# Tokens of a dilated attention put in the order of their residue modulo 4, in a two-layer decoder kernel

## The chip, the cores and the metric

One core of one Trainium2 chip runs the whole kernel in one launch. The metric is the device time of one execution in microseconds (us); lower is better.

## The reference

Two decoder layers on 256 tokens of width 1024, in float32. Each layer adds a token mixer, then a mixture of 32 experts (top 2 of one group of 8), then a gated per-layer embedding. The mixer of layer 0 is the dilated attention (DSA) that the change is in; layer 1 has latent attention (MLA), which it doesn't touch.

The DSA has 8 heads of 128 columns, and each head three groups with their own q, k and v. A query at token t sees, in group g, the keys t, t-d, t-2d, ... down to t-window:

```
DSA_PATTERNS = ((128, 1), (512, 4), (2048, 16))      # (window, dilation) per group
s = where(valid, q.k * dh**-0.5 - slope * (t - key), -inf)
```

The three groups are joined by their softmax denominators, which is the same as one softmax over all keys of the three groups. Its result goes through w_out. With 256 tokens, groups 1 and 2 see only keys whose distance is a multiple of 4 and of 16; their windows reach past the first token.

## The kernel before

All five engines have their own written-out program, tied by semaphores. TensorE multiplies, ScalarE casts and takes exponentials, VectorE subtracts, scales and normalizes, SP's queue issues the weight loads in a fixed order, and POOL's queue some small loads. PSUM has eight banks of 512 float32 columns per partition.

**Start.** The rows of x are normalized in two chunks of 128 tokens. TensorE transposes them (`turn_rows`, L1295) into banks 4 to 7. VectorE multiplies by the gain on the way out (`gains_on`, L833), which gives `hT`, the activations with the tokens along the columns. Products in the attention are done in three passes (`three_pass`, L1300 to L1302): each operand is split into a high half, made by ScalarE's cast to a one-pass type (`hT_hi` L628, `w_qk_hi` L563 and L631), and a low half, the difference, made by VectorE (`hT_lo` L932, `w_qk_lo` L857). `hT_hi` lies over `hs`, where the rows were before the transposition. TensorE's first product, L1398, waits for both chunks of `hT_hi`.

**Head loop.** While head h is attended, head h+1 is projected. TensorE's step is: `scores` of h, two of three `project_qk` of h+1, `turn` of h, the third `project_qk`, `weigh` of h, `project_v` of h+1. The queries come in two blocks of 128 tokens. Query block 0 sees key block 0, query block 1 sees both, in each of three groups: nine score blocks of 128 by 128. VectorE adds slope times distance from a table (`a_dist`; unseen keys have -1e30 there), takes the row maximum (`softmax_head`) and later scales by the reciprocal of the sum (`softmax_tail`); ScalarE takes the exponentials (`attend`). `turn` transposes the nine blocks three by three (L1353) into bank 5, bank 6 and bank 5 again; ScalarE copies out both rounds of bank 5 (L591), VectorE bank 6 (L901). `weigh` (L1364, L1367) multiplies with v into bank 7, from where ScalarE copies the head's output (L595). The last head's output is cast (L651) and subtracted (L954) right there, before the rest of the output product `mix_part`.

**After it.** Mixing, router, then 32 experts. Their 96 weight tiles of 2 MB go through a ring of eight tiles in fixed order. A tile is loaded when its place is free: the first four when the last `project_v` is done, the next four when parts of the output product are done, and from then on when the tile eight places earlier has been used, the first of them by the gate product of expert 0 (L1525). L441 is that wait in SP's queue.

Of the kernel before, what the change touches and what calls it, by code (L numbers as in the profile page):

```python
# [34 lines left out]
DSA_SCALE = DH ** -0.5  # L35

# [124 lines left out]
def distance_table():  # L161


    d = np.zeros((P, GROUPS, 2 * P), np.float32)
    delta = np.arange(P)[:, None] + P - np.arange(2 * P)[None, :]
    for g, (window, dil) in enumerate(PATTERNS):
        seen = (delta >= 0) & (delta <= window) & (delta % dil == 0)
        d[:, g] = np.where(seen, -delta, -BIG)
    return d.reshape(P, -1)
# [22 lines left out]
def build(nc, x, out, consts, distances, gains, routers, rows, p_t, dsa_w_in, dsa_w_out, mla_w_in, mla_w_qb,  # L192
          mla_w_kvb, mla_w_out, moe_w_gate, moe_w_up, moe_w_down, ple_w, ple_w_gate):
    ctx = ExitStack()
    with ctx:
# [63 lines left out]
        a_s0 = scratch(4608, GROUPS, P)  # L259
        a_s1 = scratch(4992, GROUPS, 2 * P)  # L260
        a_o = scratch(5760, HEADS, T)
        a_pT = scratch(7808, 9, P)
        a_dist = scratch(8960, GROUPS, 2 * P)
# [230 lines left out]
        def _(pool):  # L494
# [6 lines left out]
            pool.dma_start(a_dist, distances.rearrange("p (g n) -> p g n", g=GROUPS)).then_inc(S("dist_in"), 16)  # L501
# [29 lines left out]
        def _(act):  # L531
# [46 lines left out]
            def attend(h):  # L578

                act.wait_ge(S("nmx_ready"), h + 1)  # L580
                s0 = a_s0.rearrange("p g n -> p (g n)")
                s1 = a_s1.rearrange("p g n -> p (g n)")
                act.activation(s0, s0, ACT.Exp, bias=a_nmx[:, 0:1], scale=DSA_SCALE,
                               accum_out=a_den[:, 0:1]).then_inc(S("e_ready"), 1)
                act.activation(s1, s1, ACT.Exp, bias=a_nmx[:, 1:2], scale=DSA_SCALE,
                               accum_out=a_den[:, 1:2]).then_inc(S("e_ready"), 1)
# [64 lines left out]
            act.copy(a_o_hi[:, HEADS - 1, :], bank(7)[:, 0:T]).then_inc(S("o_high"), 1)  # L651
# [145 lines left out]
        def _(dve):  # L797
# [28 lines left out]
            def gains_on(i, c):  # L826
# [4 lines left out]
                for b in range(2):  # L831
                    dve.wait_ge(S("hT_turned"), 4 * i + 2 * c + b + 1)
                    dve.tensor_tensor(hT[:, 4 * b:4 * b + 4, c * P:(c + 1) * P], bank(4 + 2 * c + b, 4, P),  # L833
                                      gain[:, 4 * b:4 * b + 4].unsqueeze(2).to_broadcast([P, 4, P]),
                                      ALU.mult).then_inc(S("hT_ready"), 1)
# [39 lines left out]
            def softmax_head(h):  # L875

                dve.wait_ge(S("s_ready"), h + 1)
                for g in range(GROUPS):
                    slope = cst[:, bass.ds(C_SLOPE + GROUPS * h + g, 1)]
                    src = bank(3)[:, 2 * P * g:2 * P * g + 2 * P] if g < 2 else bank(4)[:, 0:2 * P]  # L880
                    dve.scalar_tensor_tensor(out=a_s0[:, g, :], in0=a_dist[:, g, P:2 * P], scalar=slope,
                                             in1=bank(2)[:, P * g:P * g + P], op0=ALU.mult, op1=ALU.add)
                    ins = dve.scalar_tensor_tensor(out=a_s1[:, g, :], in0=a_dist[:, g, :], scalar=slope,
                                                   in1=src, op0=ALU.mult, op1=ALU.add)
                ins.then_inc(S("s_taken"), 1)
                dve.wait_ge(S("s_taken"), h + 1)
                dve.tensor_reduce(a_mx[:, 0:1], a_s0.rearrange("p g n -> p (g n)"), AX.X, ALU.max)
                link(dve.tensor_reduce(a_mx[:, 1:2], a_s1.rearrange("p g n -> p (g n)"), AX.X, ALU.max))
                dve.tensor_scalar(a_nmx, a_mx, -DSA_SCALE, None, ALU.mult).then_inc(S("nmx_ready"), 1)

            def softmax_tail(h):
                dve.wait_ge(S("e_ready"), 2 * h + 2)
                link(dve.reciprocal(a_den, a_den))
                s0 = a_s0.rearrange("p g n -> p (g n)")
                s1 = a_s1.rearrange("p g n -> p (g n)")
                dve.tensor_scalar(s0, s0, a_den[:, 0:1], None, ALU.mult).then_inc(S("p_ready"), 1)
                dve.tensor_scalar(s1, s1, a_den[:, 1:2], None, ALU.mult).then_inc(S("p_ready"), 1)

            def copy_pT(h):
                dve.wait_ge(S("pT_ready"), 3 * h + 2)  # L900
                dve.tensor_copy(a_pT[:, 3:6, :], bank(6, 4, P)[:, 0:3, :]).then_inc(S("pT_copied_d"), 1)  # L901
# [909 lines left out]
```

## Time and profile before

| | us |
|---|---|
| median of 3 runs | 1408.62 (1408.11 to 1409.18) |
| the profiled execution | 1408.13 |
| its span, first to last instruction | 1406.3 |
| TensorE busy | 1058.0 (75%) |
| VectorE busy | 460.3 (33%) |
| ScalarE busy | 293.7 (21%) |
| attention of layer 0, from the first product to the end of the last head's weighting | about 13.4 to 276 |

The times are those of one core. Busy shares are means over stages with different limits, so each stage has to be looked at by itself: the attention of layer 0 lies in the first fifth of the span, the experts of layer 0 from about 310 to 760 us, layer 1 after that. Matmul records are shown with a duration that holds their latency (0.27 us for a small one), while the next one starts earlier; the distance between two starts is what one costs.

### The profile page before, as it was taken

To read this page: it belongs to the slowest core of one execution; us is meant where nothing else is said; L and a number is where in the kernel's file an instruction comes from. 1 tells how busy PE (TensorE), PEld (TensorE's weight loads), DVE (VectorE), ACT (ScalarE), POOL (GpSimd) and SP (SyncE) were. 2 spreads that over 40 slices of the span, in tenths; PEclk is the share of its full clock that TensorE was granted. 3 is DMA by queue.
4 is the path that set the end of the run, shared out by engine and by line. 5 is a ranking of instruction groups with operands and counts; after the bars stand their busy time and mean duration, and the time that the engine had idled before them with its cause. 6 is when DMAs were issued, how large, how long until landed. Compare 5 with 4: busy or idle time off the path is not lost.

```text
span 1406.3 us, 31000 instructions
## 1 busy us (share of the span) xinstructions
PE 1058.0 (75%) x13780; PEld 822.9 (59%) x13780; DVE 460.3 (33%) x1015; ACT 293.7 (21%) x557; POOL 7.8 (1%) x17
## 2 busy tenths in 40 slices
PE   7999999988665665766576988987666666676667
PEld 7999999866544444543454645565444444445445
DVE  5545555552111111211114675431111111112127
ACT  5433444321000000000004444201000000000016
POOL 0000000000000000000000000000000000000000
PEclk9999999999989988888888999999789989878889
DMA  9986540579999999999999740489999999999980
GB/s 278 310 220 169 149 130 0 239 310 426 426 425 426 426 427 425 426 425 426 427 426 397 282 172 1 172 340 426 423 426 426 427 425 427 425 428 425 427 361 35
DMA packets 113421, 469.87 MB, mean 334 GB/s; under 512 B 4656, under 2 KB 78528, under 8 KB 88464
## 3 DMA queue, kind: packets, MB, share of 16 engines
q1 hardware_dynamic: 112672, 465.78, 82.8%
q8 instruction: 112, 1.84, 0.5%
q0 software_dynamic: 624, 2.14, 0.5%
q14 instruction: 13, 0.11, 0.0%
HBM read 466.86 MB, written 1.05 MB: 333 GB/s over the span
## 4 chain that ended last, share of the span: by engine, by line
DMA 51%; PE 40%; DVE 4%; ACT 3%; issue 2%; DVEq 0%; SPq 0%; ACTq 0%
DMA ring<-moe_w_down 25%; DMA ring<-moe_w_up 11%; DMA ring<-moe_w_gate 10%; DMA ring<-ple_w_gate 5%; PE ps L1302 5%; PE ps L1300 5%; PE ps L1301 5%; PE ps L1525 5%; PE ps L1540 3%; PE ps L1615 3%; PE ps L1418 2%; PE ps L1570 2%; PE ps L1678 1%; PE ps L1447 1%; PE ps L1667 1%
## 5 line engine op out<-in xcount | busy, mean ns | idle before, releaser
L1525 PE MATMUL ps<-ring,scr 128*32 128x128 f32 x8192 | 277.9, 294 | 143.7 <-DMA ring<-moe_w_up 94.4
L1525 PEld LDWEIGHTS ps<-ring,scr 128*32 128x32 f32 x8192 | 242.6, 118 | 183.5 <-DMA ring<-moe_w_up 105.7
L1540 PE MATMUL ps<-ring,scr 128*32 128x256 f32 x2048 | 168.8, 483 | 139.3 <-DMA ring<-moe_w_down 123.3
L1540 PEld LDWEIGHTS ps<-ring,scr 128*32 128x32 f32 x2048 | 81.6, 132 | 203.1 <-issue 129.1
L674 ACT COPY scr<-ps 32x256 f32<-32x256 f32 x128 | 46.6, 364 | 552.3 <-PE ps L1540 551.5
L1061 DVE TENSOR_TENSOR scr<-scr,ps 128x128 f32<-128x128 f32 x64 | 23.8, 372 | 418.5 <-PE ps L1525 418.5
L1074 DVE COPY scr<-ps 32x256 f32<-32x256 f32 x128 | 53.3, 417 | 262.5 <-PE ps L1540 261.7
L1300 PE MATMUL ps<-hT_hi,w_qk_hi 128*128 128x256 f32 x368 | 105.8, 287 | 0.0
L1302 PE MATMUL ps<-hT_hi,w_qk_lo 128*128 128x256 f32 x368 | 103.9, 282 | 0.0
L1301 PE MATMUL ps<-hT_lo,w_qk_hi 128*128 128x256 f32 x368 | 103.5, 281 | 0.0
L1439 PEld LDWEIGHTS ps<-scr,hs 128*128 128x128 f32 x512 | 67.9, 214 | 19.2 <-issue 19.2
L1570 PE MATMUL ps<-scr 128*128 128x512 f32 x128 | 67.4, 675 | 15.4 <-DVE scr L1074 15.4
L667 ACT ACTIVATE scr<-ps 128x128 f32<-128x128 f32 x64 | 17.7, 277 | 276.3 <-PE ps L1525 276.3
L1439 PE MATMUL ps<-scr,hs 128*128 128x128 f32 x512 | 74.0, 303 | 0.0
L1300 PEld LDWEIGHTS ps<-hT_hi,w_qk_hi 128*128 128x128 f32 x368 | 70.0, 190 | 0.2
L1301 PEld LDWEIGHTS ps<-hT_lo,w_qk_hi 128*128 128x128 f32 x368 | 69.9, 190 | 0.2
L1302 PEld LDWEIGHTS ps<-hT_hi,w_qk_lo 128*128 128x128 f32 x368 | 69.8, 190 | 0.0
L857 DVE TENSOR_TENSOR w_qk_lo<-ring,w_qk_hi 128x2048 fp32r<-128x2048 f32 x24 | 54.9, 2291 | 44.5 <-ACT w_qk_hi L563 44.5
L1570 PEld LDWEIGHTS ps<-scr 128*128 128x128 f32 x128 | 26.1, 215 | 54.0 <-issue 28.0
L563 ACT CAST w_qk_hi<-ring 128x2048 fp32r<-128x2048 f32 x23 | 43.9, 1907 | 3.0 <-DMA ring<-dsa_w_in 3.0
L1300 PE MATMUL ps<-w_v_hi,hT_hi 128*128 128x384 f32 x128 | 43.4, 339 | 0.0
L1302 PE MATMUL ps<-w_v_hi,hT_lo 128*128 128x384 f32 x128 | 42.8, 334 | 0.0
(242 smaller groups left out, 1207.5 us busy)
## 6 DMA issues: line engine op xcount, KB each, us to landing
ring<-moe_w_gate SPq DMA_DIRECT2D x64, 2048.0 KB, 36.9
ring<-moe_w_up SPq DMA_DIRECT2D x64, 2048.0 KB, 36.1
ring<-moe_w_down SPq DMA_DIRECT2D x64, 2048.0 KB, 36.3
ring<-dsa_w_in SPq DMA_DIRECT2D x72, 512.0 KB, 6.7
ring<-ple_w_gate SPq DMA_DIRECT2D x4, 2048.0 KB, 36.4
ring<-dsa_w_out SPq DMA_DIRECT2D x2, 2048.0 KB, 14.0
ring<-mla_w_out SPq DMA_DIRECT2D x2, 2048.0 KB, 24.2
x_sb<-ple_w SPq DMA_DIRECT2D x2, 1024.0 KB, 10.8
```

The costliest lines, as they stand in the source:

```text
L563: act.copy(w_qk_hi[(GROUPS * par + g) % 2], w_qk[par][g]).then_inc(S("w_qk_high"), 1)
L674: ins = act.copy(e_y[CW * (i % GE):CW * (i % GE) + CW, T * q:T * q + T], bank(6)[CW * q:CW * q + CW, 0:T])
L857: dve.tensor_tensor(w_qk_lo[par][g], w_qk[par][g], w_qk_hi[(GROUPS * par + g) % 2].bitcast(F32), ALU.subtract).then_inc(S("w_qk_low"), 1)
L1074: ins = dve.tensor_copy(e_y[CW * (i % GE):CW * (i % GE) + CW, T * q:T * q + T], bank(6)[CW * q:CW * q + CW, 0:T])
L1300: pe.matmul(dst, w_hi, x_hi, start=first, stop=False)
L1301: pe.matmul(dst, w_hi, x_lo, start=False, stop=False)
L1302: return pe.matmul(dst, w_lo, x_hi, start=False, stop=last)
L1439: mm = pe.matmul(bank(7)[:, k * P:(k + 1) * P], hs[:, c, 4 * half + k, :], e_oneh[:, c, :], start=(c == 0), stop=(c == TC - 1))
L1525: mm = pe.matmul(bank(b)[CW * q:CW * q + CW, 0:P], xT[:, k, :], tile(t + j, KD, FF)[:, k, P * q:P * q + P], start=(k == 0), stop=(k == KD ...
L1540: mm = pe.matmul(bank(6)[CW * q:CW * q + CW, 0:T], e_hT[:, CW * j:CW * j + CW], tile(t + 2, FF // P, D)[:, j, T * q:T * q + T], start=(j = ...
L1570: mm = pe.matmul(bank(2 * c + n), e_sc[:, c * P:(c + 1) * P], e_y[:, 512 * n:512 * n + 512], start=False, stop=True, skip_group_check=True)
L1615: return pe.matmul(bank(2 * c + n), x_k[:, c, k, :] if x_k is hT_hi else x_k[:, k, c * P:(c + 1) * P], w[:, k, :], start=first, stop=last)
```

## The change

The tokens of the DSA are put in another order: position r*64 + i holds token 4i + r. A block of 128 positions then holds two of the four residues modulo 4. A query of the groups with dilation 4 and 16 sees keys of its own residue only, so its own block only. Group 0 (dilation 1) sees both blocks, in both query blocks. This makes 2 x (2 + 1 + 1) = 8 score blocks instead of nine, four per query block, and the two query blocks have one shape.

What follows in the code: the distance table has four blocks for each of the two query blocks (1024 columns instead of 768). The order is made in `gains_on`: each instruction handles one of eight k-slices of a chunk of 128 tokens and reads its bank with a step of four. The casts and subtractions that make `hT_hi` and `hT_lo` are done in two pieces per chunk, since a chunk of tokens now has its columns in both blocks. Scores go to banks 2 and 3, transposes four and four to banks 5 and 6, each with one copy. The output of a head is put back into token order when it is copied out of bank 7, so nothing changes from the mixing on.

```diff
+CLASSES = 4
+PER = T // CLASSES // TC
+SEEN = (2 * P, P, P)
+SEEN_AT = (0, 2 * P, 3 * P)
@@ distance_table
-    d = np.zeros((P, GROUPS, 2 * P), np.float32)
+    token = CLASSES * (np.arange(T) % (T // CLASSES)) + np.arange(T) // (T // CLASSES)
+    d = np.zeros((P, TC, 4 * P), np.float32)
...
+        def by_class(v, c):
+            return v.rearrange("p k (r c i) -> p k r c i", r=CLASSES, c=TC)[:, :, :, c, :]
+        def by_chunk(v, c):
+            return v.rearrange("p k (r c i) -> p k r c i", c=TC, i=PER)[:, :, :, c, :]
+        def in_order(v):
+            return v.rearrange("p (r i) -> p i r", r=CLASSES)
@@ scalar
             def attend(h):
-                act.activation(s0, s0, ACT.Exp, bias=a_nmx[:, 0:1], ...)
-                act.activation(s1, s1, ACT.Exp, bias=a_nmx[:, 1:2], ...)
+                for c in range(TC):
+                    act.activation(a_s[:, c, :], a_s[:, c, :], ACT.Exp, bias=a_nmx[:, c:c + 1], ...)
             def copy_pT(h):
-                for b in (0, 2):
-                    act.wait_ge(S("pT_ready"), 3 * h + b + 1)
-                    act.copy(a_pT[:, 3 * b:3 * b + 3, :], bank(5, 4, P)[:, 0:3, :]).then_inc(S("pT_copied_a"), 1)
+                act.wait_ge(S("pT_ready"), TC * h + 1)
+                act.copy(a_pT[:, 0:4, :], bank(5, 4, P)).then_inc(S("pT_copied_a"), 1)
             def copy_o(h):
-                act.copy(a_o[:, bass.ds(h, 1), :].rearrange("p h t -> p (h t)"),
-                         bank(7)[:, 0:T]).then_inc(S("o_copied"), 1)
+                act.copy(a_o[:, bass.ds(h, 1), :].rearrange("p h (i r) -> p (h i) r", r=CLASSES),
+                         in_order(bank(7)[:, 0:T])).then_inc(S("o_copied"), 1)
...
-            for c in range(TC):
-                act.wait_ge(S("hT_ready"), 2 * c + 2)
-                act.copy(hT_hi[:, c, :, :], hT[:, :, c * P:(c + 1) * P]).then_inc(S("hT_high"), 1)
-                if c == 0:
-                    act.wait_ge(S("first_q_in"), 16)
-                    act.copy(w_qk_hi[0][:, :, 0:DH], w_qk[0][0][:, :, 0:DH]).then_inc(S("first_q_high"), 1)
+            def high_hT(c, b):
+                return act.copy(by_chunk(hT_hi[:, b, :, :], c), by_chunk(hT[:, :, b * P:(b + 1) * P], c))
+            act.wait_ge(S("hT_ready"), 2)
+            high_hT(0, 0)
+            act.wait_ge(S("first_q_in"), 16)
+            act.copy(w_qk_hi[0][:, :, 0:DH], w_qk[0][0][:, :, 0:DH]).then_inc(S("first_q_high"), 1)
+            act.wait_ge(S("hT_turned"), 4)
+            high_hT(0, 1).then_inc(S("hT_high"), 1)
+            act.wait_ge(S("hT_ready"), 4)
+            high_hT(1, 0)
+            high_hT(1, 1).then_inc(S("hT_high"), 1)
@@ vector, gains_on
+                    if i == 0:
+                        for k in range(4 * b, 4 * b + 4):
+                            ins = dve.tensor_scalar(by_class(hT[:, k:k + 1, :], c)[:, 0, :, :],
+                                                    bank(4 + 2 * c + b, 4, P)[:, k % 4, :].rearrange(
+                                                        "p (i r) -> p r i", r=CLASSES), gain[:, k:k + 1], None, ALU.mult)
+                        ins.then_inc(S("hT_ready"), 1)
@@ vector, softmax_head
-                    dve.scalar_tensor_tensor(out=a_s0[:, g, :], ... in1=bank(2)[:, P * g:P * g + P], ...)
-                    ins = dve.scalar_tensor_tensor(out=a_s1[:, g, :], ... in1=src, ...)
+                    for c in range(TC):
+                        ins = dve.scalar_tensor_tensor(out=a_s[:, c, cols], in0=a_dist[:, c, cols], scalar=slope,
+                                                       in1=bank(2 + c)[:, cols], op0=ALU.mult, op1=ALU.add)
-                dve.tensor_reduce(a_mx[:, 0:1], a_s0.rearrange("p g n -> p (g n)"), AX.X, ALU.max)
-                link(dve.tensor_reduce(a_mx[:, 1:2], a_s1.rearrange("p g n -> p (g n)"), AX.X, ALU.max))
+                link(dve.tensor_reduce(a_mx, a_s, AX.X, ALU.max))
@@ vector, start and last head
-                dve.tensor_tensor(hT_lo[:, :, c * P:(c + 1) * P], hT[:, :, c * P:(c + 1) * P],
-                                  hT_hi[:, c, :, :].bitcast(F32), ALU.subtract).then_inc(S("hT_low"), 1)
+                for b in range(TC):
+                    ins = dve.tensor_tensor(by_chunk(hT_lo[:, :, cols], c), by_chunk(hT[:, :, cols], c),
+                                            by_chunk(hT_hi[:, b, :, :].bitcast(F32), c), ALU.subtract)
...
-            dve.tensor_tensor(a_o_lo[:, HEADS - 1, :], bank(7)[:, 0:T], a_o_hi[:, HEADS - 1, :].bitcast(F32), ...)
+            dve.tensor_tensor(a_o_lo[...].rearrange("p (i r) -> p i r", r=CLASSES), in_order(bank(7)[:, 0:T]), last, ...)
@@ tensor, scores
-                for g in range(GROUPS):
-                    pe.matmul(bank(2)[:, P * g:P * g + P], q[:, 0:P], k[:, 0:P], start=True, stop=True)
-                    mm = pe.matmul(dst, q[:, P:T], k, start=True, stop=True)
+                for c in range(TC):
+                    for g in range(GROUPS):
+                        mm = pe.matmul(bank(2 + c)[:, SEEN_AT[g]:SEEN_AT[g] + SEEN[g]], q[:, own],
+                                       k if g == 0 else k[:, own], start=True, stop=True)
@@ tensor, turn
-                pe.wait_ge(S("p_ready"), 2 * h + 2)
-                for b in range(3):
-                    if b == 2:
-                        pe.wait_ge(S("pT_copied_a"), 2 * h + 1)
...
+                for c in range(TC):
+                    pe.wait_ge(S("p_ready"), TC * h + c + 1)
+                    if not first:
+                        pe.wait_ge(S("pT_copied_d" if c else "pT_copied_a"), h)
+                    for j in range(4):
+                        mm = pe.transpose(bank(5 + c)[:, j * P:(j + 1) * P], a_s[:, c, j * P:(j + 1) * P], ident)
@@ tensor, weigh
+                for c in range(TC):
+                    keys = [(0, 0), (0, 1), (1, c), (2, c)]
+                    for j, (g, kc) in enumerate(keys):
+                        mm = pe.matmul(bank(7)[:, c * P:(c + 1) * P], a_v[buf][:, g, kc * P:(kc + 1) * P],
+                                       a_pT[:, 4 * c + j, :], start=(j == 0), stop=(j == len(keys) - 1))
```

## Rows read from the trace of the kernel before

**Rows 1.** The page: busy tenths in 40 slices, GB/s, and the chain by engine.

```profile
PE   7999999988665665766576988987666666676667
...
GB/s 278 310 220 169 149 130 0 239 310 426 426 425 426 426 427 425 426 425 426 427 426 397 282 172 1 172 340 426 423 426 426 427 425 427 425 428 425 427 361 35
...
DMA 51%; PE 40%; DVE 4%; ACT 3%; issue 2%; DVEq 0%; SPq 0%; ACTq 0%
```

**Rows 2.** Stretches: us, busy us (instructions) per engine, granted clock, DMA share, GB/s.

```profile
104.00:135.00 31.00, 30.60 (x233) 30.21 (x232) 16.55 (x20) 12.60 (x14) 0.00 (x0) 1.00 0.55 153
...
283.00:314.00 31.00, 25.82 (x248) 21.52 (x246) 16.40 (x75) 6.19 (x14) 2.33 (x3) 0.89 0.83 326
...
330.00:740.00 410.00, 267.64 (x4814) 191.75 (x4806) 72.78 (x198) 30.50 (x88) 0.00 (x0) 0.88 1.01 426
```

**Rows 3.** Waits of SP's queue before 330 us: total us, times, longest.

```profile
SPq L441 <- PE ps L1525: 22.1, 5, 13.5
```

**Rows 4.** Timeline of TensorE through head 0: start, us, engine, line.

```profile
41.78 0.60 PE L1340 MATMUL ps<-scr 128*128 128x256 f32 x2
42.22 0.39 PE L1339 MATMUL ps<-scr 128*128 128x128 f32 x2
...
54.95 0.82 PE L1353 MATMUL ps<-cst,scr 128*128 128x128 f32 x6
56.17 0.55 PE L1353 MATMUL ps<-cst,scr 128*128 128x128 f32 x3 [0.40 <-ACT scr L591]
...
62.23 0.83 PE L1364 MATMUL ps<-scr 128*128 128x128 f32 x6
62.90 1.50 PE L1367 MATMUL ps<-scr 128*128 128x128 f32 x12
```

**Rows 5.** Timeline of VectorE and ScalarE, head 0.

```profile
49.77 0.62 DVE L897 TENSOR_SCALAR scr<-scr,small 128x768 f32<-128x768 f32 x1
...
57.76 0.55 DVE L901 COPY scr<-ps 128x384 f32<-128x384 f32 x1
...
55.63 0.48 ACT L591 COPY scr<-ps 128x384 f32<-128x384 f32 x1
```

**Rows 6.** Timeline of the start, all engines.

```profile
9.08 2.84 DVE L833 TENSOR_TENSOR hT<-ps,wts 128x512 f32<-128x512 f32 x4
...
10.40 1.04 ACT L628 CAST hT_hi<-hT 128x1024 fp32r<-128x1024 f32 x1 [0.69 <-DVE hT L833]
11.35 1.04 ACT L631 CAST w_qk_hi<-ring 128x1024 fp32r<-128x1024 f32 x1
...
12.30 1.04 ACT L628 CAST hT_hi<-hT 128x1024 fp32r<-128x1024 f32 x1
...
13.39 3.78 PE L1398 MATMUL ps<-hT_hi,w_qk_hi 128*128 128x256 f32 x16 [2.20 <-ACT hT_hi L628]
```

**Rows 7.** Timelines of VectorE and ScalarE, instructions near the new ones.

```profile
43.85 0.35 DVE L881 SCALAR_TENSOR_TENSOR scr<-scr,cst,ps 128x128 f32<-128x128 f32 x1 [1.53 <-PE ps L1340]
44.11 0.47 DVE L883 SCALAR_TENSOR_TENSOR scr<-scr,cst,ps 128x256 f32<-128x256 f32 x1
...
5.92 0.68 DVE L823 TENSOR_SCALAR hs<-x_sb,small 128x512 f32<-128x512 f32 x1
...
767.72 0.59 ACT L719 CAST hT_hi<-ps 128x512 fp32r<-128x512 f32 x1 [0.24 <-PE ps L1608]
...
4.45 0.63 ACT L540 ACTIVATE scr<-x_sb 128x512 f32<-128x512 f32 x1 [2.13 <-DMA x_sb<-x]
...
5.92 1.23 ACT L544 ACTIVATE hs<-x_sb,small 128x512 f32<-128x512 f32 x1 [0.23 <-DVE small L818]
```

**Rows 8.** DMA issues before 45 us: KB each, us to landing.

```profile
scr<-distances POOLq DMA_DIRECT2D x1, 384.0 KB, 6.1
```

**Rows 9.** Timeline of TensorE at the last head.

```profile
271.62 0.55 PE L1353 MATMUL ps<-cst,scr 128*128 128x128 f32 x3 [0.24 <-ACT scr L591]
...
277.19 0.50 PE L1300 MATMUL ps<-w_out_hi,a_o_hi 128*128 128x512 f32 x1 [0.92 <-DVE a_o_lo L954]
```

More of the change, by code:

```diff
@@ L35 @@
 DSA_SCALE = DH ** -0.5
+CLASSES = 4
+PER = T // CLASSES // TC
+SEEN = (2 * P, P, P)
+SEEN_AT = (0, 2 * P, 3 * P)
+assert all(d % CLASSES == 0 for _, d in PATTERNS[1:])
 MH, NOPE, ROPE, MV = 16, 64, 32, 64
@@ L161, in distance_table @@
 def distance_table():
-    d = np.zeros((P, GROUPS, 2 * P), np.float32)
[L165 to L168, printed above, removed]
+    token = CLASSES * (np.arange(T) % (T // CLASSES)) + np.arange(T) // (T // CLASSES)
+    d = np.zeros((P, TC, 4 * P), np.float32)
+    for c in range(TC):
+        own = slice(c * P, (c + 1) * P)
+        for g, (window, dil) in enumerate(PATTERNS):
+            delta = token[own, None] - (token if g == 0 else token[own])[None, :]
+            seen = (delta >= 0) & (delta <= window) & (delta % dil == 0)
+            d[:, c, SEEN_AT[g]:SEEN_AT[g] + SEEN[g]] = np.where(seen, -delta, -BIG)
     return d.reshape(P, -1)
@@ L650, in _ @@
             act.wait_ge(S("o_ready"), HEADS)
-            act.copy(a_o_hi[:, HEADS - 1, :], bank(7)[:, 0:T]).then_inc(S("o_high"), 1)
+            act.copy(a_o_hi[:, HEADS - 1, :].rearrange("p (i r) -> p i r", r=CLASSES), in_order(bank(7)[:, 0:T])
+                     ).then_inc(S("o_high"), 1)
             def experts(l):
@@ L832, in gains_on @@
                     dve.wait_ge(S("hT_turned"), 4 * i + 2 * c + b + 1)
[L833 to L835 removed]
+                    if i == 0:
[4 more added lines that the diff above has]
+                        ins.then_inc(S("hT_ready"), 1)
+                    else:
+                        dve.tensor_tensor(hT[:, 4 * b:4 * b + 4, c * P:(c + 1) * P], bank(4 + 2 * c + b, 4, P),
+                                          gain[:, 4 * b:4 * b + 4].unsqueeze(2).to_broadcast([P, 4, P]),
+                                          ALU.mult).then_inc(S("hT_ready"), 1)
             def norm_staged(i, add, between, after=None):
@@ L953, in _ @@
             dve.wait_ge(S("o_high"), 2)
-            dve.tensor_tensor(a_o_lo[:, HEADS - 1, :], bank(7)[:, 0:T], a_o_hi[:, HEADS - 1, :].bitcast(F32),
-                              ALU.subtract).then_inc(S("o_low"), 1)
+            last = a_o_hi[:, HEADS - 1, :].bitcast(F32).rearrange("p (i r) -> p i r", r=CLASSES)
+            dve.tensor_tensor(a_o_lo[:, HEADS - 1, :].rearrange("p (i r) -> p i r", r=CLASSES), in_order(bank(7)[:, 0:T]),
+                              last, ALU.subtract).then_inc(S("o_low"), 1)
             def add_mixed(l):
@@ L1335, in scores @@
                     pe.wait_ge(S("s_taken"), h)
[L1336 to L1340 removed]
+                for c in range(TC):
+                    own = slice(c * P, (c + 1) * P)
+                    for g in range(GROUPS):
+                        q, k = a_qk[buf][:, g, 0:T], a_qk[buf][:, g, T:2 * T]
+                        mm = pe.matmul(bank(2 + c)[:, SEEN_AT[g]:SEEN_AT[g] + SEEN[g]], q[:, own],
+                                       k if g == 0 else k[:, own], start=True, stop=True)
                 mm.then_inc(S("s_ready"), 1)
             def turn(h, first=False):
[L1345 to L1353 removed]
+                for c in range(TC):
+                    pe.wait_ge(S("p_ready"), TC * h + c + 1)
[3 more added lines that the diff above has]
+                        mm = pe.transpose(bank(5 + c)[:, j * P:(j + 1) * P], a_s[:, c, j * P:(j + 1) * P], ident)
                     mm.then_inc(S("pT_ready"), 1)
@@ L1362, in weigh @@
                     pe.wait_ge(S("o_copied"), h)
-                for g in range(GROUPS):
-                    pe.matmul(bank(7)[:, 0:P], a_v[buf][:, g, 0:P], a_pT[:, g, :], start=(g == 0), stop=(g == GROUPS - 1))
-                for g in range(GROUPS):
-                    for kc in range(2):
-                        mm = pe.matmul(bank(7)[:, P:2 * P], a_v[buf][:, g, kc * P:(kc + 1) * P],
-                                       a_pT[:, 3 + 3 * kc + g, :], start=(g == 0 and kc == 0),
-                                       stop=(g == GROUPS - 1 and kc == 1))
+                for c in range(TC):
+                    keys = [(0, 0), (0, 1), (1, c), (2, c)]
+                    for j, (g, kc) in enumerate(keys):
+                        mm = pe.matmul(bank(7)[:, c * P:(c + 1) * P], a_v[buf][:, g, kc * P:(kc + 1) * P],
+                                       a_pT[:, 4 * c + j, :], start=(j == 0), stop=(j == len(keys) - 1))
                 mm.then_inc(S("o_ready"), 1)
```

44 lines of the change are left out of this document (14 added, 30 removed).

## The prediction

> **What bounds the kernel now.** I read the two strips of the page first, then the table by stretches, then the timeline of TensorE through one attention head, then the two places where TensorE is not full. The page's strip of TensorE stands at 9 for the first seven of forty slices and falls to 5 to 8 after them, while the bytes per second rise to 426 GB/s and stay there; the chain of the page is 51% DMA and 40% PE [rows 1]. So there are two regimes. The change lies in the first, the attention of layer 0. The table by stretches shows it: in the 31.0 us from 104 to 135 us, which is one head, TensorE works 30.60 us at a granted clock of 1.00 (the 2.4 GHz level), VectorE 16.55 us, ScalarE 12.60 us, and the DMA share is 0.55 [rows 2]. Everything but TensorE has more than 14 us of slack per head. A TensorE instruction taken out there moves the end of the head by its own pitch; work taken off VectorE or ScalarE moves nothing.
>
> The second regime is the experts, 330 to 740 us: DMA share 1.01 at 426 GB/s [rows 2]. What has to be seen is who starts this stream. The ring has eight tiles. Four are released by the last value projection, four by the mixing of the attention output, and the ninth load waits for the gate projection of expert 0: the SP queue's longest wait for L1525 is 13.5 us [rows 3]. Between 283 and 314 us the DMA share is 0.83, so the stream has holes until TensorE has gone through mixing, router and first gate [rows 2]. The full stream therefore starts a fixed amount of work after TensorE leaves the attention, and no transfer in it starts at a fixed time. A microsecond saved before mixing is a microsecond off the whole kernel. This is the second regime's only tie to the change, since the output is put back in token order before mixing.
>
> **Scores, per head.** Before: three products of 128 columns and three of 256. After: four of 128 and two of 256. The 256-column form (two records) starts at 41.78 and what follows it at 42.22: 0.44 us. The 128-column form is two records as well, and records of that size follow each other every 0.67/6 = 0.112 us (six from 62.23 to 62.90), so 0.22 [rows 4]. Before 3 x 0.66 = 1.98, after 2 x 0.44 + 4 x 0.22 = 1.76: saved 0.22.
>
> **Turning, per head.** Before: nine transposes into two banks, so the third group must wait until ScalarE has copied the first. Six start at 54.95 and last 0.82 with the 0.27 of the last one's own latency, a pitch of 0.11; they are issued by 55.61, and the third group starts at 56.17, released by the copy of L591 [rows 4]. The hole in the issue is 0.56 us (the row says 0.40, because it counts from the modelled end of the last transpose). After: eight transposes, four into bank 5 and four into bank 6, and the only copies waited for are those of the head before. Saved 0.56 + 0.11 = 0.67. The wait does not come back at the weighting: ScalarE's one copy of 512 columns replaces two of 384, and VectorE's copy, which stands behind the splitting of weights and starts at 57.76 for 0.55, grows by about 0.13 to 128 more columns' worth; the weighting starts at 62.23, almost 4 us later [rows 4, 5].
>
> **Weighting, per head.** Nine products of two records become eight: 18 records to 16, saved 2 x 0.112 = 0.22 [rows 4].
>
> **Softmax, per head.** VectorE adds the distances in two instructions of 256 and four of 128 columns instead of three and three: the 128 form is followed after 0.26 us (43.85 to 44.11), so it gets a little shorter [rows 7]. One reduction replaces two, the exponentials and the scalings go from 384 and 768 to 512 and 512. All of this hangs between the scores and the turning, hidden under two projections, as the 14 us of VectorE's slack per head say [rows 2]. VectorE ends the scaling at 50.4, and the turning starts at 54.95 [rows 4, 5]. I cost it at nothing; without the cover it would be a gain of one or two tenths. The head's output copy now reads its bank in another order, hidden by the same slack for all heads but the last.
>
> So a head gives 0.22 + 0.67 + 0.22 = 1.11 us, and seven heads 7.77. In the eighth, TensorE's wait in the turning is 0.24 instead of 0.40 [rows 9], so it gives 0.95. Together 8.72.
>
> **The start, which pays.** The permuted order has to be made when the transposed activations are scaled by the gain. Before: four instructions of 512 columns from 9.08 lasting 2.84 us; then ScalarE casts chunk 0 at 10.40, the first query weights at 11.35, chunk 1 at 12.30, and TensorE begins at 13.39 [rows 6]. After: sixteen instructions of 128 columns, each with a bank read in steps of four, and four casts of 512 columns instead of two of 1024 (a cast of 512 into this type took 0.59 [rows 7] and one of 1024 lasts 1.04 [rows 6], so a pair lasts 0.1 more). With a pitch p for the small instruction, chunk 1 is ready at 9.08 + 16p + 0.08; behind it stand two casts, 0.48 + 0.58, and 0.05 to TensorE: it begins at 10.27 + 16p, if that is the last thing. The trace has no such instruction. From above: L881 also reads a bank, 128 columns, and is followed after 0.26; of this 0.13 is the columns (L883 has 128 more and lasts 0.12 to 0.13 longer) and 0.13 fixed [rows 7]. p = 0.26 gives 14.43, a delay of 1.0. From below, with half of the fixed part, p = 0.20; then ScalarE's own chain is last (a cast of 512, the query weights, three casts, from 10.76: 13.8) and the delay is 0.4. With a penalty for the step: ScalarE's pass with a step of eight elements (L544) took 1.23 where a plain pass over as many columns (L540) took 0.63, a doubling by the step; VectorE's stepped form of the same work (L823) took 0.68 for 512 columns, no doubling [rows 7]. If 128 columns of a bank cost VectorE double, p = 0.39 and the delay is 3.1. A step that costs more than double has no row near it. I take 0.26, as VectorE's stepped row shows no penalty. The later waits of the first projection (the low halves of the activations, and of the first weights) belong to its second and third pass, of 16 products each, where the first pass alone lasts 3.8 us [rows 6], and the two halves of 0.6 us that VectorE now takes for each of the two chunks are done before them, so the delay counts once: +1.0, between 0.4 and 3.1.
>
> The Trainium skill speaks against this part: its page "PSUM — Partial Sum Buffer", section Specifications (TRN2), gives 8-byte cachelines and says that any non-contiguous access pattern slows matmuls significantly. It names matmuls, not VectorE, and gives no factor; no run here shows it yet. By it the dearer start would be the likelier one, which is the first rival below.
>
> **The last head's end.** L651 and then the subtraction lie bare before the mixing, with TensorE idle for 0.92 [rows 9]. Both now read the bank in steps. If ScalarE doubles per element (0.60 more for 512 columns, so 0.30 for 256 [rows 7]) this costs 0.3; nothing at the least, 0.6 if VectorE suffers too. I take +0.3.
>
> **Queues.** The distance table grows from 384 to 512 KB on POOL's queue; it landed in 6.1 us before [rows 8], and its reader is the first softmax at 43.85 [rows 7], so even with the load behind it (biases and router weights) nothing is late. SP issues the same loads under the same conditions. VectorE waits once per head for both probabilities as before.
>
> **Sum.** -7.77 - 0.95 + 1.0 + 0.3 = -7.4 us. The profiled execution took 1408.13 us, 1406.3 of span and 1.8 around it; less 7.4 it is 1400.7. The median of the runs shown is 1408.62, half a microsecond above, so for a median I say 1401.2.
>
> **Rivals.**
> First, a dear stepped read of the banks: 3.1 at the start and 0.6 at the end instead of 1.3. The gain is 8.72 - 3.7 = 5.0, the time 1403.6. For it speaks L544, against it L823 [rows 7]. 15%.
> Second, the hole in the turning is not the copy's: the time of the switch between transposes and projection stays, or the wait for the probabilities takes its place. Then a head gives 0.55, eight 4.4, less 1.3 is 3.1 and the time 1405.5. Against it: VectorE's scaling is done 4.5 us before the turning [rows 4, 5], and the row names the copy [rows 4]. 7%.
> Third, the stream of experts does not start earlier, for a load or a wait that I have not seen: the attention ends 7.4 us earlier and the DMA gives it back. The time is 1408.6. For it speaks the share of 51% for DMA [rows 1]; against it, the ninth load waits for TensorE [rows 3] and the share before 314 us is 0.83 [rows 2]. 6%.
> Fourth, the other side: the sixteen small instructions cost so much that the start eats all. With 0.6 at the last head, the sum is zero at 16p = 8.72 - 0.6 + 3.12, p = 0.70 us, and slower by 2.8 us at p = 0.88. At p = 0.9 the time would be 1411.7. It would need six times the per-column cost of L881 [rows 7]. 4%.
>
> **Chances and range.** The forecast, between 1400.0 and 1402.5, has 68%. A measurement of this kernel tells about 0.2%, 2.8 us, from no change. Forecast, first rival and most of the second are beyond it: 0.89 faster; the third and the rest of the second 0.07 same; 0.04 slower. The range goes past the first rival and almost to the second above (1405.0), and below to 1398.8, for a start that costs 0.4, a last head that costs nothing, and a microsecond of difference between executions.
>
> **What would show it.** In the profile of the changed kernel a head lasts 29.9 us instead of 31.0 with TensorE idle for nothing in the turning; the eight transposes stand in one run; the small gain instructions have a pitch near 0.26, and the first product starts near 14.4; the output cast of the last head shows its price in the idle time before the mixing; the experts' stretch shows the same 426 GB/s, only earlier by the whole sum. The prediction is wrong if the pitch at the start is twice as large, if a hole appears before the weighting, or if the stream of experts starts where it did.

## The result, and the profile after

The changed kernel takes 1398.45 us (median of 4, 1395.45 to 1399.37) against 1408.36 us (median of 4) before: ratio 0.9925, 95% interval 0.9907 to 0.9943, so 9.9 us faster, by the interval 8 to 13. The prediction said 1401.2 us, a gain of 7.4, and a range down to 1398.8. The direction and most of the sum were right; the time lies 0.35 us below the range. Two single executions of the sets below took far longer than all others, one of `pause` with 2497.1 us and one of the kernel before in the second set with 1568.7 us; without them the medians of `pause` and of that set would be 1407.40 instead of 1407.41 and 1409.1 instead of 1409.4 us.

The page of the changed kernel, the lines that answer to [rows 1]:

```profile
PE   6999999977656666666667988987666666565667
...
GB/s 285 312 223 177 160 116 0 271 350 426 425 426 427 427 426 427 426 427 426 426 427 393 291 153 1 173 372 425 427 427 426 426 427 427 426 425 427 427 371 40
...
DMA 50%; PE 41%; DVE 5%; issue 2%; ACT 2%; DVEq 0%; SPq 0%; ACTq 0%
```

The regimes are the same, and so is the 426 GB/s. The table by stretches (columns as in [rows 2]): one head, then from the end of the attention to the first SiLU of the experts, then the experts.

```profile
104.00:133.87 29.87, 29.87 (x230) 29.77 (x229) 16.20 (x18) 12.12 (x13) 0.00 (x0) 1.00 0.58 159
268.70:304.00 35.30, 28.54 (x218) 23.26 (x221) 20.35 (x83) 9.96 (x19) 2.33 (x3) 0.95 0.84 339
304.00:750.20 446.20, 299.26 (x5416) 213.33 (x5406) 82.00 (x224) 34.16 (x99) 0.00 (x0) 0.87 1.00 423
```

SP's queue still waits for the gate products of the first experts, which are L1549 here, as in [rows 3] (us in total, times, longest):

```profile
SPq L459 <- PE ps L1549: 26.2, 7, 12.7
```

A head takes 29.87 us and TensorE is busy in all of it. The timeline of TensorE in head 0, for [rows 4]:

```profile
42.95 1.92 PE L1368 MATMUL ps<-scr 128*128 128x256 f32 x12
44.62 0.37 PE L1328 MATMUL ps<-hT_hi,w_qk_hi 128*128 128x256 f32 x1
44.83 0.28 PE L1329 MATMUL ps<-hT_lo,w_qk_hi 128*128 128x256 f32 x1
...
56.14 1.03 PE L1379 MATMUL ps<-cst,scr 128*128 128x128 f32 x8
56.93 0.37 PE L1328 MATMUL ps<-hT_hi,w_qk_hi 128*128 128x256 f32 x1
57.13 0.28 PE L1329 MATMUL ps<-hT_lo,w_qk_hi 128*128 128x256 f32 x1
...
62.71 1.95 PE L1392 MATMUL ps<-scr 128*128 128x128 f32 x16
```

The eight transposes stand in one run, with no idle time named beside them. Projection products follow each other every 0.12 us, so the projection after the scores counts from 44.71 and the one after the transposes from 57.01: scores 1.76 us (predicted 1.76), turning 0.87. In the kernel before, the projection after the transposes shows these lines:

```profile
56.47 0.36 PE L1300 MATMUL ps<-hT_hi,w_qk_hi 128*128 128x256 f32 x1
56.67 0.27 PE L1301 MATMUL ps<-hT_lo,w_qk_hi 128*128 128x256 f32 x1
```

By the same reading it counts from 56.55, so nine transposes with the hole took 1.60 us from 54.95 [rows 4].

The start, all engines, for [rows 6]:

```profile
9.29 4.22 DVE L855 TENSOR_SCALAR hT<-ps,wts 128x128 f32<-128x128 f32 x16
...
11.47 0.62 ACT L640 CAST hT_hi<-hT 128x512 fp32r<-128x512 f32 x1 [1.55 <-DVE hT L855]
...
12.00 1.04 ACT L645 CAST w_qk_hi<-ring 128x1024 fp32r<-128x1024 f32 x1
12.94 1.73 ACT L640 CAST hT_hi<-hT 128x512 fp32r<-128x512 f32 x3
```

Sixteen small instructions in 4.22 us, the last with its full 0.34: a pitch of 0.26, as taken. TensorE's first product starts at 14.73, 1.34 later than before; 0.21 of it is x, which landed later in this execution (the first square at 4.66 instead of 4.45), so the price is 1.13 (predicted 1.0). From the first gain instruction to the first product it is 5.44 us instead of 4.31, which gives 1.13 again.

The last head's end, timelines of ScalarE, VectorE and TensorE, for [rows 9]:

```profile
268.67 0.37 ACT L670 CAST a_o_hi<-ps 128x256 fp32r<-128x256 f32 x1 [3.73 <-PE ps L1392]
...
269.07 0.42 DVE L982 TENSOR_TENSOR a_o_lo<-ps,a_o_hi 128x256 fp32r<-128x256 f32 x1 [3.59 <-ACT a_o_hi L670]
...
269.55 0.50 PE L1328 MATMUL ps<-w_out_hi,a_o_hi 128*128 128x512 f32 x1 [0.92 <-DVE a_o_lo L982]
```

TensorE is idle for 0.92 here, as in [rows 9], where 0.3 more was predicted. The product stands at 269.55 instead of 277.19: the attention gives 7.64 us in this pair of profiles. The medians differ by 9.9. Where the other two come from is what most of the experiments are for.

### The profile page after: what moved, and what is told of

It is laid out like the page before. It is cut to its first block, busy times and chain, and to the rows that moved or that the text cites. A ratio compares the mean times of both kernels' runs of the same rounds, so it can differ in the third digit from the quotient of the medians.

```text
span 1393.7 us, 30955 instructions
## 1 busy us (share of the span) xinstructions
PE 1054.6 (76%) x13756; PEld 814.1 (58%) x13756; DVE 459.3 (33%) x1021; ACT 290.1 (21%) x551; POOL 7.8 (1%) x17
## 4 chain that ended last, share of the span: by engine, by line
DMA 50%; PE 41%; DVE 5%; issue 2%; ACT 2%; DVEq 0%; SPq 0%; ACTq 0%
DMA ring<-moe_w_down 28%; DMA ring<-moe_w_up 11%; DMA ring<-moe_w_gate 8%; PE ps L1549 6%; PE ps L1328 5%; PE ps L1330 5%; PE ps L1329 5%; PE ps L1564 4%; PE ps L1639 3%; DMA ring<-ple_w_gate 3%; PE ps L1442 2%; PE ps L1594 2%; PE ps L1392 1%; PE ps L1368 1%; PE ps L1463 1%
## 5 line engine op out<-in xcount | busy, mean ns | idle before, releaser
L1549 PE MATMUL ps<-ring,scr 128*32 128x128 f32 x8192 | 272.4, 290 | 136.4 <-DMA ring<-moe_w_up 85.4
L1549 PEld LDWEIGHTS ps<-ring,scr 128*32 128x32 f32 x8192 | 237.0, 116 | 175.9 <-DMA ring<-moe_w_up 97.5
L1564 PE MATMUL ps<-ring,scr 128*32 128x256 f32 x2048 | 176.2, 500 | 142.5 <-DMA ring<-moe_w_down 126.7
L694 ACT COPY scr<-ps 32x256 f32<-32x256 f32 x128 | 46.6, 364 | 554.4 <-PE ps L1564 553.6
L1594 PE MATMUL ps<-scr 128*128 128x512 f32 x128 | 71.2, 707 | 15.4 <-DVE scr L1102 15.4
```

What stands on the lines that cost most here:

```text
L694: ins = act.copy(e_y[CW * (i % GE):CW * (i % GE) + CW, T * q:T * q + T], bank(6)[CW * q:CW * q + CW, 0:T])
L1549: mm = pe.matmul(bank(b)[CW * q:CW * q + CW, 0:P], xT[:, k, :], tile(t + j, KD, FF)[:, k, P * q:P * q + P], start=(k == 0), stop=(k == KD ...
L1564: mm = pe.matmul(bank(6)[CW * q:CW * q + CW, 0:T], e_hT[:, CW * j:CW * j + CW], tile(t + 2, FF // P, D)[:, j, T * q:T * q + T], start=(j = ...
L1594: mm = pe.matmul(bank(2 * c + n), e_sc[:, c * P:(c + 1) * P], e_y[:, 512 * n:512 * n + 512], start=False, stop=True, skip_group_check=True)
```

## The experiments

Three theories for the two microseconds. A: they are scatter between executions. B: the later stages take less when they lie earlier. C: the changed program is quicker later for a reason of its own. "The end of the attention" is the start of the last head's cast in one profile of each kernel. Kernels were timed in turn with the kernel before, whose median was 1408.4, 1409.4, 1407.4 and 1408.1 us in the four sets. Each set ran on another chip, so a difference to the kernel before of the same set is safer than one across sets. "The changed kernel's 1398.7 us" is the median of its ten executions, the four above and the six below.

### The same kernel again

No edit.

> The changed kernel once more, nothing altered, for more executions beside the kernel before. In the one profiled execution of it the attention ended 7.64 us earlier, while the medians differ by 9.9 us. Theory A (the other 2.3 us are differences between executions in the stages after the attention, and no work of the change): the difference comes out near 7.6 us, ratio 0.9946. Theory B (starting the later stages earlier pays more than the shift) and theory C (the changed program is quicker in stages that the change does not touch, for a reason of its own): 9.9 us again, ratio 0.993.

1398.83 us (6 executions, 1398.05 to 1399.83), ratio 0.9922 (0.9899 to 0.9944); the attention ends at 268.0. A second profile of the kernel before ends it at 275.8:

> The kernel before once more, for a second profile of it. Its attention ends at 276.3 us as in the first profile within 0.7 us. Theory A (the stages after the attention vary from execution to execution, whatever their place in time): the time from the end of the attention to the end of the span, 1130.0 us in the first profile, comes out anywhere between 1125 and 1132, the values seen for the six profiles of all kernels so far. Theory B (the place in time decides): 1130 to 1132 again, as in the three profiles whose attention ended at 272 us or later.

1408.88 us (8 executions), ratio 1.0005 (0.9987 to 1.0023). The stretch from the end of the attention to the end of the span took 1129.6 us: inside theory A's interval and 0.4 under theory B's, so one profile decides little here. The 9.6 to 9.9 us stand, and a scatter in the first four executions does not explain them.

### Nine blocks without the hole

```diff
-                    if b == 2:
-                        pe.wait_ge(S("pT_copied_a"), 2 * h + 1)
-                    elif not first:
+                    if not first:
...
+                    for n in ((0, 1, 2, 3), (4, 5, 6, 7), (8,))[b]:
...
+                        mm = pe.transpose(bank((5, 6, 4)[b])[:, at * P:(at + 1) * P], src, ident)
```

> The kernel before, still with nine blocks and the old order of tokens, but the transposes go four to bank 5, four to bank 6 and one to the free half of bank 4, so that none waits for a copy of the same head. By the prediction's term for the hole (0.56 us in seven heads, 0.40 in the last) the attention ends 4.3 us earlier and the time is 4.3 us lower than before. If the hole was not the copy's, but the switch of TensorE between transposes and projections, nothing is gained. If all gain of the change comes from the order of tokens, nothing either.

1404.1 us (12 executions), ratio 0.9963 (0.9946 to 0.9981): 4.3 us less than before, as expected; the attention ends at 272.1, 4.0 earlier. Its timeline of TensorE at the turning of head 0:

```profile
55.47 1.14 PE L1353 MATMUL ps<-cst,scr 128*128 128x128 f32 x9
56.37 0.37 PE L1301 MATMUL ps<-hT_hi,w_qk_hi 128*128 128x256 f32 x1
56.57 0.28 PE L1302 MATMUL ps<-hT_lo,w_qk_hi 128*128 128x256 f32 x1
```

Nine in one run, 0.98 us where it was 1.60. So over half of what a head gains comes from a free bank for the ninth block, and not from the order of the tokens; with eight blocks it only falls out by itself. The second rival is out.

### The start with four instructions

```diff
-                        for k in range(4 * b, 4 * b + 4):
-                            ins = dve.tensor_scalar(by_class(hT[:, k:k + 1, :], c)[:, 0, :, :], ...)
+                        dve.tensor_tensor(by_class(hT[:, 4 * b:4 * b + 4, :], c),
+                                          bank(4 + 2 * c + b, 4, P).rearrange("p k (i r) -> p k r i", r=CLASSES),
+                                          gain[:, 4 * b:4 * b + 4].unsqueeze(2).unsqueeze(3).to_broadcast(...), ALU.mult)
```

> The changed kernel, with the sixteen gain instructions of 128 columns replaced by four of 512 columns that write the permuted order themselves (four slices, four residues, 32 tokens each). If the price of the start is the fixed part of sixteen small instructions (0.13 us each), the first product starts at about 13.5 instead of 14.7 us and the time falls by 1.1 us against the changed kernel. If reading the bank in steps of four is what costs, an instruction of 512 columns lasts well over the 0.69 us that it lasted before, up to 1.3 us, and nothing is gained.

1398.01 us (6 executions, 1397.36 to 1398.14), 0.8 us below the changed kernel timed beside it, the fastest version that keeps the whole computation. Its start:

```profile
9.14 2.84 DVE L854 TENSOR_TENSOR hT<-ps,wts 128x512 f32<-128x512 f32 x4
...
10.45 0.62 ACT L640 CAST hT_hi<-hT 128x512 fp32r<-128x512 f32 x1 [0.68 <-DVE hT L854]
...
13.63 1.65 PE L1421 MATMUL ps<-hT_hi,w_qk_hi 128*128 128x256 f32 x6 [2.38 <-ACT hT_hi L640]
```

Four instructions of 512 columns, read in steps of four, take 2.84 us, exactly what the unstepped ones took [rows 6]. The step is free on VectorE; the price of the start was the number of instructions. From the first gain instruction (9.14) to the first product it is 4.49 us, against 5.44 in the changed kernel and 4.31 before: 0.95 saved of 1.13, where 1.1 was expected, in agreement with the 0.8 us of the medians. The 0.2 left are as much as the prediction put on ScalarE's four casts instead of two. Counted from the first square (4.27) it would be 0.7 saved, but in this profile the second chunk of x came 0.24 us later behind the first than in the others.

### Added and left-out work before the end of the attention

```diff
-                for c in range(TC):
+                for c in list(range(TC)) * (5 if first else 1):      # scores of head 0; 3 and 2 in the next two
```

> The changed kernel with the score products of head 0 done five times instead of once, which gives the same values: four extra sets of 1.75 us, 7.0 us of added TensorE work at the first head, with everything after it shifted as a block. Theory A: 7.0 us slower than the changed kernel, and 0.6 us faster than the kernel before. Theory B: the extra gain goes with the shift, so about 9 us slower than the changed kernel and level with the kernel before. Theory C: 7.0 us slower than the changed kernel and 2.9 us faster than the kernel before.

> The changed kernel with the score products of head 0 done three times instead of once (same values): 3.5 us of added work, attention ends at about 271.8 us. The changed kernel has its median at 1398.7, the one with 7.0 us added at 1407.4, 8.7 later. Theory A: the medians lie on a line of slope 1 within their scatter, 1402.2, at most 1403. Theory B as a step between 268 and 272 us (the kernels that end their attention after 272 need 1132 us from there to the end, those that end it before 269 need 1130.5): 1403.8.

> The changed kernel with the score products of head 0 done twice instead of once (same values): 1.75 us added, attention ends at about 270.1 us. The time less the end of the attention is 1130.4 for the kernels that end it before 269 us and 1132 to 1133.7 for those that end it after 271 us (medians of the executions, less the profiled end of the attention). Theory A (scatter only): 1400.5, on the line of slope 1 through the changed kernel. Theory B (the place in time of the later stages decides): between 1400.5 and 1403, by where the step lies.

Measured 1407.41, 1405.00 and 1402.38 us (12 executions each). Against the changed kernel's 1398.7 that is 8.7 for 7.0 us of added work, 6.3 for 3.5 and 3.7 for 1.75. The second lies 1.2 above even theory B's 1403.8. Between the three the slope is 5.0 for 5.25. The first 1.75 us cost two more than themselves. All three have the changed program, and all three are slower than it by more than their work, which speaks against theory C. These are differences across sets; against the kernel before of their own sets the three are 1.0, 4.4 and 5.0 us faster.

```diff
+                        if isinstance(h, int) and h < 2:             # project_v of heads 0 and 1
+                            pe.matmul(dst, hT_hi[:, c, k, :], w_v_hi[:, k, :], start=(k == 0), stop=False)
+                            mm = pe.matmul(dst, hT_hi[:, c, k, :], lo[:, k, :], start=False, stop=(k == KD - 1))
```

> The kernel with the fast start; in addition the product of the low half of the activations with the weights is left out of the value projection of heads 0 and 1, which changes the result slightly: 32 products of 0.173 us, 5.5 us less of TensorE work, attention ends near 262 us. Its median so far is 1398.0. Theory A: 1392.5. Theory B, if each microsecond of shift gives 1.2 to 1.3: 1391 or less. If the gain in the later stages is a floor already reached: 1392.5 or more.

1392.25 us (6 executions): 5.8 less than the kernel with the fast start, which was timed in another set, for 5.5 of work and an attention end 6.1 earlier, slope 1. No further gain, no floor.

> The kernel before, nine blocks and the old order, but with TensorE work left out so that its attention ends where that of the changed kernel does: the product of the low activations with the weights in the value projection of heads 0 and 1 (32 products of 0.173 us, 5.5 us), and the product of the low half of the output with the weights in the first 17 steps of the output product (17 of 0.233 us, 4.0 us). This changes the result slightly. The attention ends near 266.8 us. Theory B: the later stages take what they take behind the changed kernel, 1130.5 us, so the time is 1397.3. Theory C (the changed program itself is quicker later): 1132.5 us as for the kernel before, so 1399.3. Theory A: anything between.

1397.23 us (6 executions), the number of theory B. Its attention ends at 266.6. But the kernel before timed beside it had 1407.4: the difference is 10.1 us, by the interval 7.7 to 13.4, for an attention end 9.4 earlier. Slope 1 without any step lies inside that interval too, so this run alone doesn't separate B from C.

> The kernel before with the score products of head 0 done three times (same values): 4.0 us added, attention ends at 280.1 us. Theory A and C: 1408.7 + 4.0 = 1412.7. Theory B, if there is one step between 268 and 272 us and none later: 1412.7 too; if each microsecond of shift costs 1.2 to 1.3: 1413.7.

1411.94 us (10 executions), attention end 279.4. It is 4.6 us above the kernel before of its set, by the interval 1.8 to 6.2, for 4.0 of work: slope 1 on this side too, as far as this resolves it.

All twelve, in the order of the end of the attention. The third number is the median less that end; the fourth is the time of the profiled execution alone less its end of the attention; the last is from that end to the first sigmoid of the embedding gate, in the one profile:

```
kernel                 attention end   median   median - end   same execution   to first sigmoid
before_late                279.4       1411.9      1132.5          1134.0            501.9
before (first profile)     276.3       1408.4      1132.1          1131.8            502.4
before_again               275.8       1408.9      1133.1          1131.4            504.9
pause                      275.0       1407.4      1132.4          1133.5            503.9
nine_no_hole               272.1       1404.1      1132.0          1133.9            503.3
pause_half                 271.3       1405.0      1133.7          1134.2            504.9
pause_one                  269.9       1402.4      1132.5          1132.7            505.3
changed                    268.7       1398.45     1129.8          1126.8            500.7
again                      268.0       1398.8      1130.8          1130.1            503.6
fast_start                 267.4       1398.0      1130.6          1130.0            502.0
before_early               266.6       1397.2      1130.6          1131.6            500.0
ahead                      261.3       1392.2      1130.9          1130.0            501.6
```

By the medians, the seven kernels that end the attention at 269.9 us or later need 1132.0 to 1133.7 from there, the five that end it by 268.7 need 1129.8 to 1130.9. The groups don't overlap, and each holds both programs: before_early is the program before, the pauses are the changed one. That speaks against plain scatter and, by the pauses, against C. It is not proof. The border between the groups was put between 268 and 272 us after the first six profiles, and narrowed by the later runs; the ratios of single kernels have intervals of 2 to 3 us to each side; and a line of slope 1.15 through all twelve misses the medians by 0.9 us (root mean square), where two levels of slope 1 miss them by 0.5. Within single executions (fourth column) the groups are 1131.4 to 1134.2 and 1126.8 to 1131.6, so they touch, and the program before shows no step there: 1131.8 and 1131.4 unshifted, 1131.6 in before_early.

### Added work in layer 1

```diff
-                for k in range(KD):                                  # latents of chunk 0, layer 1
+                for k in list(range(KD)) * (1 if c else 2):
```

> The changed kernel with the latent projection of the first 128 tokens of layer 1 done twice (same values): eight products of 416 columns in four passes each, 5.5 us by an estimate from the 0.44 us of a 256-column product, some of it perhaps beside a wait. The attention of layer 0, the experts of layer 0 and the embedding gate stay where they are; everything from the latents on moves. If the two microseconds that kernels with an attention end after 269 us lose are lost before the latents, the time is 1398.7 plus the added work as the profile shows it. If they are lost in the latent attention, the router or the experts of layer 1, some two more.

1404.56 us (12 executions). The stretch up to the latents grew from 5.6 to 11.1 us in the profile, so 5.5 was added, and 1399.1 is left. Its line in the timeline of TensorE, 32 matmul records where there were 16:

```profile
786.26 11.33 PE L1702 MATMUL ps<-ring,hT 128*128 128x416 f32 x32
```

```diff
+                if (l, c, n) == (1, 0, 0) and 0 in ks:
+                    for k in range(4):
+                        pe.matmul(bank(0), m_o[:, k, rows], tile(Tiles.MLA_OUT, KD, 512)[:, k, :], start=(k == 0), stop=(k == 3))
```

> The changed kernel with four more steps of the output product of layer 1 ahead of the first (their result is overwritten, same values): four products of 512 columns, 3.5 us by the same estimate. Only the router and the experts of layer 1 move. If the two microseconds are lost before the router of layer 1: 1402.2. If in it or in the experts of layer 1: 1404.2.

1402.61 us (6 executions): less 3.5 it is 1399.1 as well. Both are within 0.4 of the changed kernel; measured against the kernel before of their own set they are 0.5 to 0.9 slower than that, which the runs don't resolve. Their attention ends early, at 268.0 and 268.6, and less the added work they need 1131.1 and 1130.5 from there, near the early group. So most of the two microseconds are not lost when only what lies behind the latents moves; they are decided before it: in the router and experts of layer 0, or the embedding gate. The last column of the table agrees: 500.0 to 503.6, mean 501.6, for the early group, 501.9 to 505.3, mean 503.8, for the late one; but these overlap, with one profile each.

The same profiles can be split at the last copy of the experts (L674 before, L694 in the changed kernel). With the two new runs among the early ones, the way from the end of the attention to that copy takes 481.5 to 483.4 us, mean 482.4, early, and 481.3 to 484.6, mean 482.8, late. From there to the first sigmoid, in the embedding gate, it is 17.8 to 22.1, mean 19.6, early, and 19.5 to 22.0, mean 21.0, late. So as far as one profile each can tell, more of the difference lies in the gate than in the experts.

What such a stretch varies by can be seen. From the end of the attention to the first SiLU, in fast_start and in before_early:

```profile
267.40:304.30 36.90, 31.36 (x220) 25.50 (x223) 20.48 (x83) 10.03 (x20) 2.34 (x3) 0.86 0.81 325
```

```profile
266.60:301.00 34.40, 28.33 (x213) 23.41 (x217) 20.29 (x83) 10.00 (x19) 2.33 (x3) 0.90 0.93 380
```

The changed kernel's own profile has 35.30 us at 0.95 (above), so 1.6 us lie between granted clocks of 0.86 and 0.95 for the same work, fast_start and the changed kernel being the same program in this stretch. The clock is not all of it: before_early is shorter than both at 0.90, with 380 GB/s where they have 325 and 339. The same at the end of the experts, TensorE in the kernel before and in the changed one, the last rows of down projection and scatter:

```profile
755.21 1.93 PE L1540 MATMUL ps<-ring,scr 128*32 128x256 f32 x32 [1.31 <-DMA ring<-moe_w_down]
758.10 3.70 PE L1570 MATMUL ps<-scr 128*128 128x512 f32 x8 [0.96 <-DVE scr L1074]
```

```profile
746.90 2.90 PE L1564 MATMUL ps<-ring,scr 128*32 128x256 f32 x32 [2.74 <-DMA ring<-moe_w_down]
750.75 5.57 PE L1594 MATMUL ps<-scr 128*128 128x512 f32 x8 [0.95 <-DVE scr L1102]
```

The eight products take 3.70 us in one, at a granted clock of 1.00, and 5.57 in the other, at 0.66, and this other is the faster kernel. So one such burst took 1.9 us longer where part of it ran at the lower of the two clock levels (1.2 instead of 2.4 GHz). That the step of two microseconds is made of this is argued from such rows, not shown; and why it should depend on the place in time stays open.

## Why the prediction was wrong, point by point

- **Scores, turning, weighting.** 0.22 + 0.67 + 0.22 = 1.11 per head. Measured 0.20 + 0.73 + 0.23 by the two timelines. The distance between heads is (252.36 - 43.11)/7 = 29.89 us between the scores of head 0 and head 7, and (259.23 - 72.95)/6 = 31.05 before between those of head 1 and head 7, both by the chain; 1.15 per head. 0.3 us more in all. Right, and the hole by itself gave the 4.3 us that its term said.
- **The start.** 1.0 taken, 1.13 measured, from a pitch of 0.26 as taken. Here the Trainium skill's line on 8-byte cachelines ("PSUM — Partial Sum Buffer", Specifications (TRN2)) had been weighed as the rival with 15%: it speaks of matmuls, and the traces show that it doesn't carry over to VectorE's reads, 2.84 us with and without the step, nor to ScalarE's, 0.37 us for the last cast before and after. The first rival is out, and with the pitch of 0.26 the fourth.
- **The last head.** +0.3 taken, 0 measured: idle 0.92 in both. I had carried a doubling over from a stepped read of SBUF by ScalarE (L544) to a bank of PSUM.
- **Queues.** The distance table of 512 KB landed in 6.6 us instead of 6.1 [rows 8], and no idle time of TensorE in head 0 shows it. Right.

```profile
scr<-distances POOLq DMA_DIRECT2D x1, 512.0 KB, 6.6
```

- **The stream of experts.** It moved with TensorE, at 426 GB/s: the first SiLU of the experts starts at 304.0 instead of 312.4 us. The third rival is out.
- **The attention's part of the sum.** -7.4 was taken, -7.64 measured in the profiles. That it comes so near is in part luck: 0.3 more from the heads and 0.3 less at the last head's end stand against 0.13 more at the start and x landing 0.21 later.
- **The step that failed:** "A microsecond saved before mixing is a microsecond off the whole kernel." The prediction's sum has no term for what the later stages do when they start earlier. With the profiled attention ends of both pairs (276.3 and 275.8, 268.7 and 268.0) the attention gave 7.7 us, and the time fell by 9.6 to 9.9: the stages after the attention gave about two more. By the medians of the twelve kernels the sentence holds at slope 1 on either side of a place between 268.7 and 269.9 us, and this change moved the end of the attention past it, from 276 to 268 us. Where the two microseconds go is narrowed to the stages before the latents of layer 1; their cause stays open. The range had one microsecond for "difference between executions", where the executions of the kernel before alone lay between 1402.4 and 1416.0 us in the first set of experiments.

## What to carry to other kernels

Where one engine is full, count its pitches and its holes; the sum of eight heads came out within 0.3 us. Look at a hole apart from the change that happens to close it: a free half bank ended the attention 4.0 of the 7.7 us earlier without reordering anything. And when the first stage of a kernel like this one shrinks, allow the later ones the couple of microseconds that they moved here; the range has to hold that even when the sum is right.

## What the runs showed of the hardware

- A bank of PSUM read in steps of four elements costs VectorE nothing (four instructions of 512 columns, 2.84 us in both forms), and read in steps of 64 it costs ScalarE nothing (256 columns, 0.37 us in both), though a step of eight elements in SBUF took ScalarE 1.23 instead of 0.63 us [rows 7].
- A small VectorE instruction on 128 columns of a bank has a pitch of 0.26 us, sixteen of them 4.22 us, while four of 512 take 2.84.
- The same work in the 35 us after the attention took 1.6 us longer at a granted clock of 0.86 than at 0.95. The medians less the end of the attention are about 2 us lower in the kernels whose attention ends before 269 us; this was not expected and is not explained.
